# Later modulation pieces in the first bodies of three phases, and an earlier wait for the context latent

## The chip, the cores and the metric

The kernel runs on one core of one Trainium2 chip. The metric is the device time of one execution in microseconds; the comparison is between the medians of several executions of the kernel before and of the changed one.

## What is computed

All arithmetic is float32 on 256 tokens of width 2048. Two blocks follow one another. Cut to what matters here:

```python
# first block
h = x + hybrid_mixer(rms_norm(x), w_in, ...)                  # ends with @ w_out
h = h + memory_cross_attention(rms_norm(h), rms_norm(mem), wq, wk, wv, wo)
h = h + square(relu(rms_norm(h) @ mlp_w1)) @ mlp_w2
x = rms_norm(h)
# second block: its modulation depends on c, c_ctx and w_mod alone, not on x
sh1, sc1, gt1, sh2, sc2, gt2 = split(silu(c) @ w_mod + b_mod, 6)
csh1, csc1 = first two of split(silu(c_ctx) @ w_mod + b_mod, 6)
h  = rmsnorm(x) * (1 + sc1) + sh1
hc = rmsnorm(ctx) * (1 + csc1) + csh1
cq, ckv, kr, qn, kn, vn, f = split_columns(h @ w_in)
ckv_c, kr_c, kn_c, vn_c = those columns of hc @ w_in
kv_c = rmsnorm(ckv_c, g_kv) @ w_ukv                           # "context latent"
...                                                           # attentions, fourier mix, conv_ffn
```

`w_mod` is 2048 x 12288. Because the product with it needs nothing of the first block, it is computed beside the first block's big matrix products.

## The kernel before, in words

All weight matrices lie in one stream of 906 **slots** of 128 x 1024 float32 (512 KB), in the order in which they are used. A **phase** (`Phase`, in the table `PH`) is one matrix product over a run of slots. A **block** of a phase is 256 output columns; for a product over 2048 inputs it has 4 slots. Phases run in **bodies**: memk, memv, wq, wo and all w1 and w2 phases have two bodies of 16 slots each.

Each slot passes through five hands, in this order on each of them:

- SyncE (`load`, L362) brings it from HBM into one of 8 `raw` buffers, once the slot eight earlier has been split.
- ScalarE (`slot`, L1015) rounds it to the upper part `whi`, one of 4 buffers, once TensorE has done the slot four earlier.
- VectorE (`slot`, L1597) subtracts: lower part `wlo` = `raw` - `whi`.
- TensorE (`phase`, L485) does 24 matmuls on a slot: weights upper x input upper, upper x lower, lower x upper.
- ScalarE and VectorE take the finished block out of PSUM (`evac_fn` in `over`), three slots later (`LAG`).

Nothing but the order of the instructions on each engine sets the schedule. `over` writes that order for ScalarE and VectorE. It makes the first three slots (`PRE`) of a phase in the **tail** of the phase before, beside the steps called `tail(j)`. In the tails of wout, memv and wo these steps are the normed input of the next phase: ScalarE makes an upper quarter of `act` (L1106, `upper_after`), VectorE the lower quarter (L1703, `lower_after`), four of them. wout and wo are residual phases: the block taken out is added to `h` (L1654) and squared by ScalarE (L1093); the squares are summed on VectorE (L1642, L1723). The last quarter on ScalarE is queued behind the last square, and the upper parts of slots 3 to 6 of the next phase behind that quarter. TensorE starts slot n of the first block only with quarter n of the input and with its own `wlo`.

**The modulation.** The product with `w_mod` runs over 24 bodies, those of memk to w2_3. In each, VectorE makes 16 **pieces** (`mod_chunk`): a piece multiplies 128 x 512 of `w_mod` by one column of silu(c) and adds it to `modacc`; piece 0 is L1581, the others L1583. In the 8 bodies of memk to wo a piece is done twice, once for c and once for c_ctx; in the w1 and w2 bodies once. The table `MOD_AT` says which pieces stand at which slot of a body; the first piece of an entry stands ahead of that slot's `wlo`, the others behind it. From the second modulated body on, piece 0 comes behind a copy of the last body's result out of PSUM (L1560). TensorE sums `modacc` over the partitions behind slot 12 of the body (L505, `MOD_OUT_AT`), once piece 15 is done.

Two pieces share one load of 512 KB into one of two `modraw` buffers (L368). On SyncE's queue one such load follows every two loads of slots, and it waits until the pair of pieces two earlier is done (`mod_used`). SyncE works in order, so a waiting modulation load holds up the slots behind it.

GpSimd issues a load of 2 MB, the context (L404), when the first block of w1_0 has been taken out.

**The context latent.** In the second block, `ckv_c` normed is the input of phase kn_c, slots 588 to 591. ScalarE makes its upper part (`latent_upper`, L1438) and VectorE its lower part (`latent_lower`, L2219), both in the tail of kr_x behind the third slot made ahead for kn_c (j = 2). They go to chunks 0 to 3 of `act`. kr_x, the phase before, has two slots of 8 chunks each: the first reads chunks 0 to 7 of `act`, the second chunks 8 to 15. In that tail VectorE also has `latent_part(2)` (L2195), the sum of the squares of another latent.

```python
MOD_AT = ((0, 1), (2,), (3,), (4,), (5,), (6,), (7,), (8, 9), (10,), (11,), (12,), (13,), (14,), (15,))
...
for k in ks[:1]:
    mod_chunk(ph, i, k)
ve.wait_ge(hi_done, i * ph.S + (at + 1))
ve.tensor_tensor(wlo[...], raw[...], whi[...], ALU.subtract).then_inc(split_done, 1)
for k in ks[1:]:
    mod_chunk(ph, i, k)
```

Of the kernel before, what the change touches and what calls it, by code (L numbers as in the profile page):

```python
# [37 lines left out]
RAW_N, SPL_N, MOD_N = 8, 4, 2  # L38
# [55 lines left out]
MOD_BODIES = 24  # L94
MOD_CTX = 8
MOD_AT = ((0, 1), (2,), (3,), (4,), (5,), (6,), (7,), (8, 9), (10,), (11,), (12,), (13,), (14,), (15,))

MOD_OUT_AT = 12
PRE = 3
PH, N_SLOTS = phases()  # L100
# [26 lines left out]
def build(nc, x_t, mem_t, ctx_t, stream, mods, pvec, eye, cmix, catt, na_bias, na_mask, out_t):  # L127
    es = ExitStack()
    with es:
# [3 lines left out]
        def sem(name):  # L133
            return es.enter_context(nc.semaphore(name))
# [101 lines left out]
        slot_used = sem("slot_used")  # L236
# [768 lines left out]
        def _(sc):  # L1005
# [429 lines left out]
            def latent_upper(n, c0, src):  # L1435

                sc.wait_ge(lat_normed, n + 1)
                sc.activation(act[:, 0, c0:c0 + LC, :], src, ACT.Copy).then_inc(lat_hi, 1)  # L1438
# [62 lines left out]

            def context_latent_upper(j):
                if j == 2:
                    sc.wait_ge(slot_used, SPL_N + PH["kr_x"].slot0 + PH["kr_x"].slots)
                    latent_upper(0, 0, ckv[:, 1, :, :])
            phase("ckv_c", to(ckv[:, 1, :, :]), both_sqrt)
            phase("kr_c", one(kr[:, 1, :]), second_sqrt)
# [15 lines left out]
            phase("ckv_x", to(ckv[:, 0, :, :]), local("ckv_x"), into("cq"))  # L1523
            phase("cq", to(cq), local("cq"), into("kr_x"))
            phase("kr_x", one(kr[:, 0, :]), local("kr_x"), into("kn_c", context_latent_upper))
            phase("kn_c", to(kN[:, :, 1, :]), local("kn_c"), into("v_c"))
            phase("v_c", to(mlaV[:, 1, :, :], flip=True), local("v_c"), into("kn_x"))
# [18 lines left out]
        def _(ve):  # L1546
# [15 lines left out]
            def mod_chunk(ph, i, k):  # L1562

                mb = i + ph.mod0
                q = k // 2
                if k % 2 == 0:
                    ve.wait_ge(mod_in[q % MOD_N], mb * 64 + 16 * (q // MOD_N + 1))
                if k == 0:
                    if mb:
                        mod_store(mb, 2 if mb <= MOD_CTX else 1)  # L1570
                elif k % 2 == 0:
                    ve.wait_ge(mod_used, mb * 8 + (k // 2 + MOD_N))
                else:
                    ve.wait_ge(dve_step, mod_mark[k - 1])
                for w in range(ph.mod):
                    wt = modraw[:, q % MOD_N, (k % 2) * MOD_COL:(k % 2 + 1) * MOD_COL]
                    at = C_SILU + DC * w + k
                    col = small[:, at:at + 1]
                    acc = modacc[:, w, :]
                    if k == 0:  # L1580
                        ins = ve.tensor_scalar(acc, wt, col, None, ALU.mult)  # L1581
                    else:
                        ins = ve.scalar_tensor_tensor(acc, wt, col, acc, ALU.mult, ALU.add)  # L1583
                if k % 2:
                    ins.then_inc(mod_used, 1)
                else:
                    chain.tick(ins)
                    mod_mark[k] = chain.now()

            def slot(ph):  # L1590
                def f(i, j):
                    at = ph.slot0 + j
                    ks = MOD_AT[j] if ph.mod and j < len(MOD_AT) else ()
                    for k in ks[:1]:
                        mod_chunk(ph, i, k)
                    ve.wait_ge(hi_done, i * ph.S + (at + 1))
                    ve.tensor_tensor(wlo[:, at % SPL_N, :], raw[:, at % RAW_N, :], whi[:, at % SPL_N, :].bitcast(F32),  # L1597
                                     ALU.subtract).then_inc(split_done, 1)
                    for k in ks[1:]:
                        mod_chunk(ph, i, k)  # L1600
                return f
# [879 lines left out]
```

## Time and profile before

| | us |
|---|---|
| median of 3 runs | 2903.57 |
| lowest, highest | 2901.63, 2904.53 |
| the profiled execution, its own time | 2901.38 |
| span of its trace | 2899.6 |
| TensorE busy | 2817.0 |
| VectorE busy | 2066.1 |
| ScalarE busy | 1357.9 |

The profiled execution took 1.8 us more than its span, which lies outside the trace. Times of rows count from the start of the span. In the trace PE is TensorE, DVE VectorE, ACT ScalarE, POOL GpSimd, and SPq the queue of SyncE. In a timeline the columns are start, duration, engine, line, operation, what it writes from what, shape and count, and in brackets the idle time ahead of it and who ended it. Two instructions of an engine overlap a little in the records: a `wlo` lasts 1.22 us, but the next instruction is shown to start 1.13 us after it.

### The profile page before, as it was taken

Reading aid. Unit: us, or ns where it says so; the run is one execution under the profiler, and the core shown is the slowest. Engines: PE = TensorE matmul, PEld = TensorE weight load, DVE = VectorE, ACT = ScalarE, POOL = GpSimd, SP = SyncE. Lnnn points to the kernel's source line nnn. Section 1 sums busy time; section 2 is a strip of 40 time slices with the busy share of each in tenths; the row PEclk is TensorE's granted clock in tenths of the full one; section 3 lists DMA queues with packets and bytes.
Section 4 is the critical chain, followed back from the end, with each engine's and each line's share of the span. In section 5 each row is a group of like instructions: output and inputs, shape, how many; then the busy total and the mean of one; then the engine's idle time right before and its main releaser. Section 6 shows DMA issues by size and latency. Waiting matters only on the chain.

```text
span 2899.6 us, 55174 instructions
## 1 busy us (share of the span) xinstructions
PE 2817.0 (97%) x23814; PEld 2768.6 (95%) x23814; DVE 2066.1 (71%) x2866; ACT 1357.9 (47%) x1723; POOL 4.6 (0%) x12
## 2 busy tenths in 40 slices
PE   7999998999999999999999999999989999999998
PEld 7999998999999999999999999997789999999998
DVE  7988755888869787787777866545566665675675
ACT  4445453444434553544545545455445544553453
POOL 0000000000000000000000000000000000000000
PEclk9999998999999999999999999999999999999999
DMA  6555204678747777777777765433245566556553
GB/s 237 182 175 165 68 8 155 209 275 288 261 152 250 288 279 279 285 282 283 293 275 273 277 219 189 163 122 124 89 149 199 194 198 191 194 188 201 191 188 124
DMA packets 160516, 591.59 MB, mean 204 GB/s; under 512 B 17840, under 2 KB 17840, under 8 KB 159760
## 3 DMA queue, kind: packets, MB, share of 16 engines
q1 hardware_dynamic: 159408, 580.45, 57.9%
q0 software_dynamic: 864, 7.60, 0.7%
q8 instruction: 188, 3.08, 0.4%
q14 instruction: 56, 0.46, 0.1%
HBM read 585.88 MB, written 2.10 MB: 203 GB/s over the span
## 4 chain that ended last, share of the span: by engine, by line
PE 88%; DVE 7%; ACT 2%; issue 1%; DMA 1%; SPq 0%; DVEq 0%; ACTq 0%
PE bank L485 79%; DVE wlo L1597 2%; PE bank L827 1%; DVE modacc L1583 1%; PE bank L690 1%; PE bank L505 1%; ACT whi L1015 1%; PE bank L704 1%; PE bank L522 1%; PE bank L526 1%; PE bank L795 1%; PE bank L805 1%; DVE tmp L1776 0%; PE bank L794 0%; PE bank L514 0%
## 5 line engine op out<-in xcount | busy, mean ns | idle before, releaser
L485 PE MATMUL bank<-act,whi 128*128 128x256 f32 x10144 | 1765.2, 280 | 44.3 <-DVE wlo L1597 28.7
L485 PEld LDWEIGHTS bank<-act,whi 128*128 128x128 f32 x10144 | 1546.3, 190 | 50.2 <-DVE wlo L1597 25.8
L1597 DVE TENSOR_TENSOR wlo<-raw,whi 128x1024 fp32r<-128x1024 f32 x906 | 1096.5, 1222 | 453.0 <-ACT whi L1015 450.9
L485 PE MATMUL bank<-act,wlo 128*128 128x256 f32 x5072 | 1413.9, 279 | 0.0
L1015 ACT ACTIVATE whi<-raw 128x1024 fp32r<-128x1024 f32 x906 | 943.3, 1057 | 779.2 <-PE bank L485 778.5
L485 PEld LDWEIGHTS bank<-act,wlo 128*128 128x128 f32 x5072 | 962.5, 190 | 0.0
L485 PE MATMUL bank<-hid,whi 128*128 128x256 f32 x3456 | 590.2, 277 | 1.5 <-DVE wlo L1597 1.5
L485 PEld LDWEIGHTS bank<-hid,whi 128*128 128x128 f32 x3456 | 520.8, 188 | 1.9 <-DVE wlo L1597 1.3
L485 PE MATMUL bank<-hid,wlo 128*128 128x256 f32 x1728 | 478.2, 277 | 0.0
L1583 DVE SCALAR_TENSOR_TENSOR modacc<-modraw,small,modacc 128x512 f32<-128x512 f32 x480 | 348.3, 746 | 18.9 <-DMA modraw<-mods 13.6
L485 PEld LDWEIGHTS bank<-hid,wlo 128*128 128x128 f32 x1728 | 324.9, 188 | 0.0
L485 PE MATMUL bank<-whi,act 128*128 128x256 f32 x896 | 156.8, 279 | 0.2 <-ACT kN L1027 0.2
L485 PEld LDWEIGHTS bank<-whi,act 128*128 128x128 f32 x896 | 136.3, 188 | 0.5 <-ACT kN L1027 0.4
L485 PE MATMUL bank<-wlo,act 128*128 128x256 f32 x448 | 124.6, 278 | 0.0
L1679 DVE SCALAR_TENSOR_TENSOR ev<-bank,pv,ev 128x255 f32<-128x255 f32 x176 | 76.9, 478 | 63.2 <-ACT ev L1080 61.6
L1832 DVE SCALAR_TENSOR_TENSOR modacc<-cin,pv,modacc 128x256 f32<-128x256 f32 x232 | 98.4, 477 | 0.0
L485 PEld LDWEIGHTS bank<-wlo,act 128*128 128x128 f32 x448 | 84.1, 188 | 0.0
L1093 ACT ACTIVATE ev<-h 128x512 f32<-128x512 f32 x32 | 20.2, 632 | 124.1 <-DVE h L1654 78.8
L1080 ACT ACTIVATE ev<-bank,pv 128x256 f32<-128x256 f32 x88 | 44.9, 560 | 70.6 <-PE bank L485 70.6
L1668 DVE TENSOR_TENSOR hid<-ev,hid 128x512 fp32r<-128x512 f32 x32 | 22.1, 692 | 64.9 <-ACT hid L1069 64.9
L1085 ACT ACTIVATE ev<-ev 128x256 f32<-128x256 f32 x44 | 18.4, 418 | 80.1 <-DVE ev L1679 80.1
L1066 ACT ACTIVATE ev<-bank 128x512 f32<-128x512 f32 x32 | 19.1, 598 | 53.2 <-PE bank L485 53.2
(363 smaller groups left out, 1519.5 us busy)
## 6 DMA issues: line engine op xcount, KB each, us to landing
raw<-stream SPq DMA_DIRECT2D x906, 512.0 KB, 4.6
modraw<-mods SPq DMA_DIRECT2D x192, 512.0 KB, 4.5
h<-x_t SPq DMA_DIRECT2D x4, 512.0 KB, 5.2
memV<-mem_t POOLq DMA_DIRECT2D x1, 2048.0 KB, 8.5
tmp<-ctx_t POOLq DMA_DIRECT2D x1, 2048.0 KB, 9.7
out_t<-tmp SPq DMA_DIRECT2D x4, 512.0 KB, 2.6
cz<-catt POOLq DMA_DIRECT2D x1, 1216.0 KB, 11.6
bias<-na_bias POOLq DMA_DIRECT2D x1, 1024.0 KB, 5.2
```

The source lines that it names most:

```text
L485: mm = pe.matmul(b[:, hf * T:(hf + 1) * T], lhs, rhs, start=(kc == 0 and hf == 0 and n == 0), stop=(kc == ph.chunks - 1 and n == 2), skip_ ...
L505: mm = pe.matmul(bank[2][:, 4 * w + n:4 * w + n + 1], modacc[:, w, n * P:(n + 1) * P], ones[:, 0:1], start=True, stop=True, skip_group_che ...
L522: return pe.matmul(out, src[:, tok], ones[:, 0:1], start=start, stop=stop, skip_group_check=True)
L526: return pe.matmul(out, small[:, col + n:col + n + 1].to_broadcast([P, P]), ident[:, :], start=start, stop=True, skip_group_check=True)
L690: mm = pe.matmul(bk(hg, 0)[:, n, :], MT[hg][:, n, :], X[hg][:, n, :], start=True, stop=True)
L704: mm = pe.matmul(bk(hg, 2)[:, n, :], XT[hg][:, n, :], Y[hg][:, n, :], start=True, stop=True)
L1015: sc.activation(whi[:, at % SPL_N, :], raw[:, at % RAW_N, :], ACT.Copy).then_inc(hi_done, 1)
L1080: ins = sc.activation(ev[:, 0, hf * T:(hf + 1) * T], b2(b)[:, hf, :], ACT.Identity, scale=par("ff_conv", n * 6 + (6 * first + 3 * hf + 1)) ...
L1583: ins = ve.scalar_tensor_tensor(acc, wt, col, acc, ALU.mult, ALU.add)
L1597: ve.tensor_tensor(wlo[:, at % SPL_N, :], raw[:, at % RAW_N, :], whi[:, at % SPL_N, :].bitcast(F32), ALU.subtract).then_inc(split_done, 1)
L1679: ins = ve.scalar_tensor_tensor(o, b2(b)[:, hf, so], par("ff_conv", n * 6 + (6 * first + 3 * hf + j)), o, ALU.mult, ALU.add)
L1832: ins = ve.scalar_tensor_tensor(acc, x_, w, acc, ALU.mult, ALU.add)
```

## The change

`MOD_LATE` names memk, wq and w1_0. In their first body the pieces follow a second table: none stands at slots 0 to 2, and the 16 pieces stand at slots 3 to 13, two at some of them. Their second bodies and all other phases keep `MOD_AT`.

In the tail of kr_x, ScalarE's upper part of the context latent waits for the first slot of kr_x instead of for both.

```diff
 MOD_AT = ((0, 1), (2,), (3,), (4,), (5,), (6,), (7,), (8, 9), (10,), (11,), (12,), (13,), (14,), (15,))
+MOD_LATE = {"memk", "wq", "w1_0"}
+MOD_LATE_AT = ((), (), (), (0, 1), (2, 3), (4,), (5, 6), (7,), (8, 9), (10,), (11, 12), (13,), (14,), (15,))
...
             def context_latent_upper(j):
                 if j == 2:
-                    sc.wait_ge(slot_used, SPL_N + PH["kr_x"].slot0 + PH["kr_x"].slots)
+                    sc.wait_ge(slot_used, SPL_N + PH["kr_x"].slot0 + 1)
                     latent_upper(0, 0, ckv[:, 1, :, :])
...
                     at = ph.slot0 + j
-                    ks = MOD_AT[j] if ph.mod and j < len(MOD_AT) else ()
+                    table = MOD_LATE_AT if ph.name in MOD_LATE and i == 0 else MOD_AT
+                    ks = table[j] if ph.mod and j < len(table) else ()
```

Instructions move on VectorE alone; the order on TensorE, ScalarE, SyncE and GpSimd is the same. In the changed kernel the lines stand two or three further down: the `wlo` line is L1600 there, the piece L1585, the lower quarter L1706, the residual L1657.

VectorE in the tail of wout and the first slots of memk, before: from the `wlo` of slot 0 of memk on.

```order
L1597 TENSOR_TENSOR wlo<-raw,whi 128x1024
L1583 SCALAR_TENSOR_TENSOR modacc<-modraw,small,modacc 128x512 x2
L1703 TENSOR_TENSOR act<-tmp,act 128x1024
L1583 SCALAR_TENSOR_TENSOR modacc<-modraw,small,modacc 128x512 x2
L1597 TENSOR_TENSOR wlo<-raw,whi 128x1024
L1703 TENSOR_TENSOR act<-tmp,act 128x1024
L1583 SCALAR_TENSOR_TENSOR modacc<-modraw,small,modacc 128x512 x2
L1597 TENSOR_TENSOR wlo<-raw,whi 128x1024
L1703 TENSOR_TENSOR act<-tmp,act 128x1024
L1654 TENSOR_TENSOR h<-bank,h 128x512
```

And now, from the lower quarter behind the same `wlo` to the `wlo` of slot 4:

```order
L1706 TENSOR_TENSOR act<-tmp,act 128x1024
L1600 TENSOR_TENSOR wlo<-raw,whi 128x1024
L1706 TENSOR_TENSOR act<-tmp,act 128x1024
L1600 TENSOR_TENSOR wlo<-raw,whi 128x1024
L1706 TENSOR_TENSOR act<-tmp,act 128x1024
L1657 TENSOR_TENSOR h<-bank,h 128x512
L1645 TENSOR_TENSOR stat<-stat,ev 128x512
L1706 TENSOR_TENSOR act<-tmp,act 128x1024
L1726 TENSOR_TENSOR stat<-stat,ev 128x512
L1583 TENSOR_SCALAR modacc<-modraw,small 128x512 x2
L1600 TENSOR_TENSOR wlo<-raw,whi 128x1024
L1585 SCALAR_TENSOR_TENSOR modacc<-modraw,small,modacc 128x512 x4
```

The four pieces that stood ahead of the residual add now stand behind it, and behind them two pieces, not one, lie between some neighbouring `wlo`.

VectorE in the first body of w1_0, before: from the last lower quarter to the `wlo` of slot 5.

```order
L1703 TENSOR_TENSOR act<-tmp,act 128x1024
L1723 TENSOR_TENSOR stat<-stat,ev 128x512
L1583 SCALAR_TENSOR_TENSOR modacc<-modraw,small,modacc 128x512
L1597 TENSOR_TENSOR wlo<-raw,whi 128x1024
L1583 SCALAR_TENSOR_TENSOR modacc<-modraw,small,modacc 128x512
L1597 TENSOR_TENSOR wlo<-raw,whi 128x1024
L1583 SCALAR_TENSOR_TENSOR modacc<-modraw,small,modacc 128x512
L1597 TENSOR_TENSOR wlo<-raw,whi 128x1024
```

And now, the same stretch from the sum behind that quarter on:

```order
L1726 TENSOR_TENSOR stat<-stat,ev 128x512
L1562 COPY msum<-bank 128x2x4
L1583 TENSOR_SCALAR modacc<-modraw,small 128x512
L1600 TENSOR_TENSOR wlo<-raw,whi 128x1024
L1585 SCALAR_TENSOR_TENSOR modacc<-modraw,small,modacc 128x512 x2
L1600 TENSOR_TENSOR wlo<-raw,whi 128x1024
L1585 SCALAR_TENSOR_TENSOR modacc<-modraw,small,modacc 128x512 x2
L1600 TENSOR_TENSOR wlo<-raw,whi 128x1024
```

The copy of the last result and piece 0 moved to slot 3, where piece 4 stood.

## Rows read from the trace of the kernel before

**Rows 1.** The page's busy times; a piece of the chain that ended last

```profile
PE 2817.0 (97%) x23814; PEld 2768.6 (95%) x23814; DVE 2066.1 (71%) x2866; ACT 1357.9 (47%) x1723; POOL 4.6 (0%) x12
...
1049.50 43.54 PE bank L485 x384
```

**Rows 2.** TensorE's waits over the span: total, times, longest

```profile
PE bank L485 <- DVE wlo L1597: 30.2, 16, 7.7
```

**Rows 3.** Timeline of VectorE, first body of memk

```profile
543.28 0.88 DVE L1581 TENSOR_SCALAR modacc<-modraw,small 128x512 f32<-128x512 f32 x2
...
554.86 0.68 DVE L1654 TENSOR_TENSOR h<-bank,h 128x512 f32<-128x512 f32 x1
...
557.26 1.23 DVE L1703 TENSOR_TENSOR act<-tmp,act 128x1024 fp32r<-128x1024 f32 x1 [1.12 <-ACT act L1106]
...
560.33 1.22 DVE L1597 TENSOR_TENSOR wlo<-raw,whi 128x1024 fp32r<-128x1024 f32 x1
...
562.79 1.22 DVE L1597 TENSOR_TENSOR wlo<-raw,whi 128x1024 fp32r<-128x1024 f32 x1
...
585.61 1.41 DVE L1583 SCALAR_TENSOR_TENSOR modacc<-modraw,small,modacc 128x512 f32<-128x512 f32 x2
```

**Rows 4.** Timeline of TensorE, same body; the stretch 561.40 to 564.80 with its clock (0.50)

```profile
561.61 0.80 PE L485 MATMUL bank<-act,whi 128*128 128x256 f32 x2 [3.54 <-DVE wlo L1597]
...
591.71 1.84 PE L505 MATMUL bank<-ones,modacc 128*128 128x1 f32 x16
...
561.40:564.80 3.40, 3.19 (x15) 3.19 (x16) 3.40 (x6) 0.00 (x0) 0.00 (x0) 0.50 0.26 84
```

**Rows 5.** Timeline of ScalarE, same body

```profile
555.57 0.63 ACT L1093 ACTIVATE ev<-h 128x512 f32<-128x512 f32 x1 [6.76 <-DVE h L1654]
...
557.06 3.88 ACT L1015 ACTIVATE whi<-raw 128x1024 fp32r<-128x1024 f32 x4
```

**Rows 6.** Timelines of VectorE and (last row) TensorE, first body of wq

```profile
732.02 0.17 DVE L1560 COPY msum<-bank 128x8 f32<-128x8 f32 x1 [1.77 <-PE bank L505]
...
742.54 2.35 DVE L1703 TENSOR_TENSOR act<-tmp,act 128x1024 fp32r<-128x1024 f32 x2
...
764.54 1.41 DVE L1583 SCALAR_TENSOR_TENSOR modacc<-modraw,small,modacc 128x512 f32<-128x512 f32 x2 [0.90 <-DMA modraw<-mods]
...
768.34 1.22 DVE L1597 TENSOR_TENSOR wlo<-raw,whi 128x1024 fp32r<-128x1024 f32 x1
...
770.51 0.39 PE L485 MATMUL bank<-act,whi 128*128 128x256 f32 x2
```

**Rows 7.** First body of w1_0: VectorE, TensorE, GpSimd, SyncE; 986 to 996 with DMA rate last

```profile
969.00 1.22 DVE L1703 TENSOR_TENSOR act<-tmp,act 128x1024 fp32r<-128x1024 f32 x1 [2.06 <-ACT act L1106]
...
986.71 0.75 DVE L1583 SCALAR_TENSOR_TENSOR modacc<-modraw,small,modacc 128x512 f32<-128x512 f32 x1 [5.17 <-DMA modraw<-mods]
...
972.68 0.50 PE L485 MATMUL bank<-act,whi 128*128 128x256 f32 x2 [2.48 <-DVE wlo L1597]
...
1000.80 0.40 PE L485 MATMUL bank<-act,whi 128*128 128x256 f32 x2
...
976.62 0.53 POOL L404 DMA_DIRECT2D tmp<-ctx_t  x1 [523.25 <-ACT ev L1066]
...
977.36 0.33 SPq L368 DMA_DIRECT2D modraw<-mods  x1
...
986.00:996.00 10.00, 9.39 (x80) 9.21 (x79) 9.21 (x12) 5.40 (x7) 0.00 (x0) 1.00 1.03 392
```

**Rows 8.** Tail of kr_x and start of kn_c: ScalarE, VectorE, TensorE

```profile
1925.91 1.06 ACT L1438 ACTIVATE act<-ckv 128x1024 fp32r<-128x1024 f32 x1 [0.33 <-PE bank L485]
...
1926.75 1.91 DVE L2195 TENSOR_REDUCE tmp<-tmp 128x256 f32<-128x1024 f32 x1
1928.57 1.22 DVE L2219 TENSOR_TENSOR act<-ckv,act 128x1024 fp32r<-128x1024 f32 x1
...
1929.85 0.56 PE L485 MATMUL bank<-act,whi 128*128 128x256 f32 x2 [3.98 <-DVE act L2219]
```

## The prediction, made before the changed kernel ran

> **What bounds the kernel now.** Start with the busy times on the page: TensorE works 2817.0 of 2899.6 us [rows 1], so only its idle time, some 82 us, can be won by reordering. Next, its waits by releaser: 30.2 us of idle are 16 waits of L485 for a lower part on VectorE [rows 2]. Then the timelines show where those waits are and what VectorE did in them. The pace of TensorE is in the chain: 384 matmuls, 16 slots, take 43.54 us, 2.72 per slot [rows 1].
>
> First body of memk: TensorE waits 3.54 us for the lower part of slot 3 [rows 4], and in the 3.4 us after the wait its granted clock is 0.50, 1.2 GHz [rows 4]. The wait comes from VectorE. It reaches the residual add L1654 at 554.86 [rows 3], though the last slot of wout left TensorE near 549.6 (from the wait's start at 558.07 back by three slots of 2.72 and by 0.22, a gap too small for a row). Behind the add hang ScalarE's square at 555.57, its last quarter, and the upper parts from 557.06 [rows 5], then VectorE's last quarter at 557.26 and the lower part of slot 3 at 560.33 [rows 3]. Ahead of the add stand four modulation pieces.
>
> First body of wq: TensorE does not wait. Slot 11 gets its lower part at 768.34 + 1.22 = 769.56 and starts at 770.51 [rows 6], so 0.95 us is left. First body of w1_0: a wait of 2.48 us at slot 3 and a wait of VectorE of 5.17 us for a modulation load [rows 7]. Start of kn_c: 3.98 us for the lower part of the context latent [rows 8].
>
> **Prices of the parts.** A doubled piece with the `wlo` behind it takes 562.79 - 560.33 = 2.46 us [rows 3]. Two quarter subtractions, the same size as a `wlo`, end 2.35 after the start of the first with 1.22 for the last, so one takes 1.13 [rows 6]. A doubled piece is then 1.33, a single one half, 0.67. Piece 0 doubled is 0.79 (shown as 0.88, less the overlap of 0.09) [rows 3].
>
> **memk, first body.** Pieces 0 to 3 leave the tail: 0.79 + 3 x 1.33 = 4.78 us. The add comes at 554.86 - 4.78 = 550.1, behind the end of wout, so the whole shift is usable. The last quarter follows at 557.26 - 4.8 = 552.5, its sum of squares 1.13 later, then piece 0 (0.79, new there in place of a piece of 1.33) and the lower part of slot 3 from 555.0 to 556.2. TensorE is ready for slot 3 at about 557.8, so the 3.54 goes, with 0.22 of an earlier gap of the same sort. The half clock goes too: 3.4 us at half speed lost 1.7. Together 5.5 us.
>
> What is late next is VectorE. Between 543.28 and piece 15 it is idle for only 1.12 us, at the last quarter [rows 3], and that wait for ScalarE stays. The work to the end of piece 15 is the same, so piece 15 still ends at 585.61 + 1.33 = 586.9. The pieces moved behind slot 3 push the lower parts of slots 5, 7, 9 and 11 past TensorE's need. The lower part of slot 12 stands ahead of piece 15 and behind piece 14 in both tables; it ends near 585.7, TensorE does the slot in 2.72 and comes to the modulation sum at about 588.7, where it stood at 591.71 [rows 4]. So 3.0 us remain. I take 0.4 off for loads (below): **-2.6**. Bounds: -5.5, if VectorE were never late, and 0, if loads eat the rest.
>
> **wq, first body.** Here nothing is to be won and VectorE loses head start: while TensorE works through the tail, VectorE now waits for upper parts where it did pieces. Pieces can begin only behind the last quarter, which ends at 742.54 + 2 x 1.13 = 744.8, or 1.33 earlier, 743.5, without the piece ahead of it. From there to the `wlo` of slot 11 stand the copy (0.08), piece 0, pieces 1 to 13 and the `wlo` of slots 3 to 10: 0.08 + 0.79 + 13 x 1.33 + 8 x 1.13 = 27.2, so that `wlo` runs 770.7 to 771.9, against a need at 770.5 [rows 6]. Loss 1.5 us. **Loads** come on top. A pair of pieces has one modulation load, and two loads of slots are queued behind it on SyncE, three of 524 KB. At slots 3 to 8 VectorE wants a pair each 3.8 us (2 pieces and a `wlo`); the old table wanted one each 4.9 (two `wlo`). At the rate of 392 GB/s of 986 to 996 [rows 7] the three take 4.0 us. Four such intervals lose 0.2 each, and before there was already one wait of 0.90 for a load in this body [rows 6], which had slack to hide in and now has none. Loads: +0.8. **wq +2.3**, bounds 0 (slack as before) and +5 (each of four loads 0.9 late).
>
> The Trainium skill, page "DMA: Bandwidth & Descriptors", section "Specifications", puts the HBM limit of a core at about 358 GB/s. By that the three loads would take 4.4 us, 0.6 late at four intervals, and wq and memk would each cost about 1.6 us more: a sum of +4.1 instead of +0.9. The trace's 392 GB/s over ten microseconds is above that figure, so I go by the trace.
>
> **w1_0, first body.** Pieces are single. The copy and pieces 0 to 3 leave the tail: 0.08 + 0.39 + 3 x 0.67 = 2.5 us. The last quarter moves from 969.00 [rows 7] to 966.5, and behind it, with the sum, copy and piece 0, the lower part of slot 3 is ready near 969.9; TensorE is ready at 972.68 - 2.48 = 970.2 [rows 7]. The 2.48 goes, just. Slower here is SyncE: the load for pair 2 can leave only after piece 1, now behind slot 3's `wlo`, near 970.6, that for pair 3 near 973.1, pair 4 near 976.7 and pair 5 near 980; pair 5's left at 977.36 [rows 7]. GpSimd's 2 MB of context is issued at 976.62 [rows 7], and now about 977.0, since the upper part of slot 6, whose load is later, stands ahead of the take-out that releases it. Beside it pair 5's load landed 9.3 us after issue, just ahead of the piece at 986.71 that waited 5.17 us for it [rows 7]. Now pair 4's and its two slots are caught by it as well. I expect piece 8 near 986.5 and slot 8 on TensorE at 988 to 989, due at 984.7; then pair 5, three transfers of 1.3 us behind, makes slot 9 wait another microsecond. Slot 12 starts at 1001 to 1005, where it stood at 1000.80 [rows 7]. **+1.2**, bounds -3.1 (2.48 and the 0.6 us by which slot 8 was late go, nothing comes) and +4.2.
>
> **kr_x.** ScalarE's order is unchanged; L1438 stands behind the upper part of the third slot and was idle for just 0.33 us ahead of it [rows 8]. That much earlier it starts. But the lower part L2219 begins at 1928.57 because VectorE is in L2195 until then (1926.75 and 1.91 long); L1438 had ended at 1926.97 [rows 8]. The queue ahead of L2219 ends the wait, not L1438. **0.0**; bounds 0 and -0.33.
>
> **Sum.** -2.6 + 2.3 + 1.2 + 0 = +0.9 us. On the profiled execution (2901.38, that is the span and 1.8) this gives 2902.3; that execution was 2.2 below the median of the three runs, so the median goes to 2903.57 + 0.9 = **2904.5**.
>
> **Rivals.**
> - *Nothing is given back.* memk -5.5, wq 0, w1_0 -3.1: -8.6, 2895. It needs VectorE to have room in memk and wq; 1.12 us idle in 43 us [rows 3] and 0.95 us of lead [rows 6] speak against. 0.04.
> - *The latent was held by ScalarE.* If the order on VectorE were not what holds L2219, the 3.98 and about 1.7 of half clock behind it would go: 0.9 - 5.7 = -4.8, 2899. Against it stand L2195's own two rows. The change then also does what its words say, which I hold it does not in effect. 0.04.
> - *Slower: loads set the pace of the pieces.* Place: SyncE's queue in the three first bodies. If three transfers take 5.0 us at the tight intervals instead of 4.0, each of four intervals costs 1.2 instead of 0.2: memk and wq 4 more each, w1_0 at its bound 4.2: 0.9 + 8 + 3 = +12, 2915. It decides from about 4.5 us per three loads (+5.8 in all). For: a load landed 9.3 us after its issue with the context beside it, and one wait of 0.90 stood in wq at the slow pace. Against: 392 GB/s. 0.12.
> - The forecast: 0.80, from 2898.5 to 2909.5 by the bounds taken together.
>
> **How the numbers follow.** About 0.2%, 5.8 us, is what a measurement of this kernel can tell from no change. The forecast and the latent rival lie within it, but for 0.01 at either edge of the forecast; the first rival is faster, the last slower. Faster 0.05, same 0.82, slower 0.13. The range for 8 in 10 leaves out the far rivals: 2899 to 2910.
>
> **What would show it.** In the changed profile: no wait of TensorE at slot 3 of memk and no half clock there, but small waits of 0.2 to 1.1 us at slots 5 to 11, and the modulation sum near 588.7; waits at slots 9 and 11 of wq, sum 2 us later against slot 0; in w1_0 no wait at slot 3, one of 3 to 4 us at slot 8; at kn_c the same 4 us. The prediction is wrong if VectorE shows idle time between the pieces of memk other than for loads, or if the modulation waits for loads exceed about 4 us in memk and wq together.

## The result

| | us |
|---|---|
| kernel before, median of 17 runs | 2904.97 (2900.83 to 2907.60) |
| changed kernel, median of 17 runs | 2909.81 (2905.97 to 2913.78) |
| ratio of the two, 95% interval | 1.0018 (1.0012 to 1.0025) |
| profiled execution of the changed kernel, its own time | 2907.19 |
| span of its trace | 2905.4 |

The ratio is +5.2 us, and its interval excludes no change. The forecast was a loss of 0.9 us, one that a measurement would not tell from no change. The sign is right, the loss is nearly six times as large, and it is clear of the scatter. The median lies 0.2 us inside the range of 2899 to 2910.

Two rows of the changed kernel's page and of its waits over the span, TensorE's busy time and its waits for lower parts (total, times, longest), against [rows 1, 2]:

```profile
PE 2818.1 (97%) x23814; PEld 2768.2 (95%) x23814; DVE 2067.7 (71%) x2866; ACT 1357.9 (47%) x1723; POOL 4.6 (0%) x12
```

```profile
PE bank L487 <- DVE wlo L1600: 34.7, 21, 8.3
```

The busy times agree with those before to within 2 us; the waits for a `wlo` grew from 30.2 us in 16 to 34.7 in 21. The loss is best read stage by stage. The table has the time from the start of slot 0 to the start of slot 12 on TensorE, each from the first matmul of the slot in the trace:

| first body of | before | after | difference | predicted |
|---|---|---|---|---|
| memk | 39.72 | 38.41 | -1.31 | -2.6 |
| wq | 32.65 | 35.80 | +3.15 | +2.3 |
| w1_0 | 38.92 | 41.99 | +3.07 | +1.2 |

At kn_c nothing changed. The sum is +4.9; the rest of the 5.8 us between the two profiled executions is small differences ahead of memk (0.5 by slot 0) and between the stages. Times of rows of the changed kernel are read against those of before after subtracting what it is ahead or behind at the start of the stage: +0.50 in memk, -0.71 in wq, +2.73 in w1_0, +5.87 at kn_c.

**memk.** Timeline of VectorE in the changed kernel, from the residual add to the first pieces; its order is that of the prediction, its times within 0.1 us of it:

```profile
550.58 0.68 DVE L1657 TENSOR_TENSOR h<-bank,h 128x512 f32<-128x512 f32 x1
...
552.98 1.23 DVE L1706 TENSOR_TENSOR act<-tmp,act 128x1024 fp32r<-128x1024 f32 x1 [1.12 <-ACT act L1108]
...
555.52 1.22 DVE L1600 TENSOR_TENSOR wlo<-raw,whi 128x1024 fp32r<-128x1024 f32 x1
556.65 2.92 DVE L1585 SCALAR_TENSOR_TENSOR modacc<-modraw,small,modacc 128x512 f32<-128x512 f32 x4
559.49 1.22 DVE L1600 TENSOR_TENSOR wlo<-raw,whi 128x1024 fp32r<-128x1024 f32 x1
```

The add, 554.86 before [rows 3], stands at 550.58 - 0.50 = 550.1, the `wlo` of slot 3 begins at 555.0 where it began at 560.33. The wait of 3.54 and the half clock behind it [rows 4] are gone. Then the stretch of slot 3 (its columns: busy time of PE, PEld, DVE, ACT, POOL, then granted clock, DMA share, GB/s), and the modulation sum on TensorE:

```profile
558.20:561.90 3.70, 3.70 (x35) 3.70 (x34) 3.70 (x5) 0.00 (x0) 0.00 (x0) 1.00 0.76 279
```

```profile
591.00 1.84 PE L507 MATMUL bank<-ones,modacc 128*128 128x1 f32 x16
```

The sum is at 591.00 - 0.50 = 590.5, not at 588.7: of the 3.0 us that VectorE's work was to leave, 1.8 are gone. One row shows where a part of them went: four instructions, two doubled pieces, take 559.49 - 556.65 = 2.84, not 2 x 1.33 = 2.66. The waits of the body:

```profile
PE bank L487 <- DVE wlo L1600: 2.5, 3, 1.1
...
DVE modacc L1585 <- DMA modraw<-mods: 1.0, 2, 0.6
```

**wq.** VectorE from piece 0 on, against [rows 6], and TensorE at slots 9 and 11:

```profile
742.87 0.88 DVE L1583 TENSOR_SCALAR modacc<-modraw,small 128x512 f32<-128x512 f32 x2
743.65 1.22 DVE L1600 TENSOR_TENSOR wlo<-raw,whi 128x1024 fp32r<-128x1024 f32 x1
744.79 2.93 DVE L1585 SCALAR_TENSOR_TENSOR modacc<-modraw,small,modacc 128x512 f32<-128x512 f32 x4
747.64 1.22 DVE L1600 TENSOR_TENSOR wlo<-raw,whi 128x1024 fp32r<-128x1024 f32 x1
...
759.60 1.42 DVE L1585 SCALAR_TENSOR_TENSOR modacc<-modraw,small,modacc 128x512 f32<-128x512 f32 x2 [0.39 <-DMA modraw<-mods]
...
771.36 1.22 DVE L1600 TENSOR_TENSOR wlo<-raw,whi 128x1024 fp32r<-128x1024 f32 x1
...
772.98 1.41 DVE L1585 SCALAR_TENSOR_TENSOR modacc<-modraw,small,modacc 128x512 f32<-128x512 f32 x2 [0.40 <-DMA modraw<-mods]
```

```profile
766.18 0.50 PE L487 MATMUL bank<-act,whi 128*128 128x256 f32 x2 [0.82 <-DVE wlo L1600]
772.63 0.50 PE L487 MATMUL bank<-act,whi 128*128 128x256 f32 x2 [0.74 <-DVE wlo L1600]
```

From piece 0 to the `wlo` of slot 11 VectorE takes 771.36 - 742.87 = 28.5, where the prediction counted 27.1 without loads. Slot 11 starts at 772.63 + 0.71 = 773.3 instead of 770.51: 2.8 late.

**w1_0.** VectorE, TensorE, SyncE and GpSimd, against [rows 7]:

```profile
969.07 1.23 DVE L1706 TENSOR_TENSOR act<-tmp,act 128x1024 fp32r<-128x1024 f32 x1 [2.07 <-ACT act L1108]
...
971.28 1.22 DVE L1600 TENSOR_TENSOR wlo<-raw,whi 128x1024 fp32r<-128x1024 f32 x1
...
990.67 0.75 DVE L1585 SCALAR_TENSOR_TENSOR modacc<-modraw,small,modacc 128x512 f32<-128x512 f32 x1 [5.58 <-DMA modraw<-mods]
...
995.18 1.22 DVE L1600 TENSOR_TENSOR wlo<-raw,whi 128x1024 fp32r<-128x1024 f32 x1
```

```profile
979.04 0.33 SPq L370 DMA_DIRECT2D modraw<-mods  x1
979.50 0.53 POOL L406 DMA_DIRECT2D tmp<-ctx_t  x1 [527.25 <-ACT ev L1068]
992.70 0.76 PE L487 MATMUL bank<-act,whi 128*128 128x256 f32 x2 [4.54 <-DVE wlo L1600]
```

The wait at slot 3 is gone. The load for pair 4, issued at 979.04, 0.46 us ahead of the 2 MB of context, lets piece 8 begin only at 990.67, 11.6 us later, and slot 8 waits 4.54 us. Behind that wait the clock falls (stretch of slot 8, columns as above):

```profile
992.60:997.60 5.00, 4.90 (x24) 4.93 (x25) 3.78 (x6) 3.10 (x5) 0.00 (x0) 0.53 1.00 394
```

Slot 8 takes 4.95 us. The `wlo` of slot 9 had ended at 995.18 + 1.22 = 996.4; slot 9 starts at 997.65, so here the half clock itself cost 1.25.

**kn_c.** Upper part, sum of squares, lower part, TensorE, against [rows 8]:

```profile
1931.35 1.05 ACT L1440 ACTIVATE act<-ckv 128x1024 fp32r<-128x1024 f32 x1
```

```profile
1932.62 1.90 DVE L2198 TENSOR_REDUCE tmp<-tmp 128x256 f32<-128x1024 f32 x1
1934.44 1.21 DVE L2222 TENSOR_TENSOR act<-ckv,act 128x1024 fp32r<-128x1024 f32 x1
```

```profile
1935.71 0.62 PE L487 MATMUL bank<-act,whi 128*128 128x256 f32 x2 [3.97 <-DVE act L2222]
```

ScalarE's upper part starts 0.4 us earlier (1925.48 against 1925.91), the lower part where it did (1928.57), and the wait is 3.97.

### The profile page after: what moved, and what is told of

It is laid out like the page before. It is cut to its first block, busy times and chain, and to the rows that moved or that the text cites. A ratio compares the mean times of both kernels' runs of the same rounds, so it can differ in the third digit from the quotient of the medians.

```text
span 2905.4 us, 55175 instructions
## 1 busy us (share of the span) xinstructions
PE 2818.1 (97%) x23814; PEld 2768.2 (95%) x23814; DVE 2067.7 (71%) x2866; ACT 1357.9 (47%) x1723; POOL 4.6 (0%) x12
## 4 chain that ended last, share of the span: by engine, by line
PE 86%; DVE 9%; ACT 2%; DMA 2%; issue 1%; SPq 0%; DVEq 0%; ACTq 0%
PE bank L487 76%; DVE wlo L1600 3%; DVE modacc L1585 2%; PE bank L829 1%; DMA modraw<-mods 1%; PE bank L692 1%; PE bank L507 1%; ACT whi L1017 1%; DVE ev L1619 1%; PE bank L706 1%; PE bank L524 1%; PE bank L528 1%; PE bank L797 1%; DVE modacc L1835 1%; PE bank L807 1%
## 5 line engine op out<-in xcount | busy, mean ns | idle before, releaser
L1600 DVE TENSOR_TENSOR wlo<-raw,whi 128x1024 fp32r<-128x1024 f32 x906 | 1096.1, 1221 | 458.2 <-ACT whi L1017 456.1
L1585 DVE SCALAR_TENSOR_TENSOR modacc<-modraw,small,modacc 128x512 f32<-128x512 f32 x480 | 348.1, 746 | 19.8 <-DMA modraw<-mods 14.2
```

## The experiments

All kernels keep the line numbers of the kernel before. Each gives one execution's trace beside the times. "Late" is the second table of the change. Stage times are again from slot 0 to slot 12.

### One part of the change at a time

Late pieces in memk alone, in wq alone, in w1_0 alone, each with the old wait for the latent; then the new wait alone, with an empty set. The first of the four against the changed kernel:

```diff
-MOD_LATE = {"memk", "wq", "w1_0"}
+MOD_LATE = {"memk"}
...
-                    sc.wait_ge(slot_used, SPL_N + PH["kr_x"].slot0 + 1)
+                    sc.wait_ge(slot_used, SPL_N + PH["kr_x"].slot0 + PH["kr_x"].slots)
```

> Late pieces in memk's first body alone; wq, w1_0 and the latent's wait as before. Theory A (each body pays its own sum, and what it costs is loads: memk -1.3, wq +3.2, w1_0 +3.3 in the changed kernel's trace, added up to its +5.2): memk reaches the modulation sum behind slot 12 at 590.4 to 591, 1 to 1.5 us sooner than before counted from memk's slot 0, nothing else moves, the time is 1.3 us below the kernel before. Rival B (what is won in memk is lost later whatever the other bodies do, since VectorE falls behind): the gain at the modulation sum is gone by the end of wo, and the time is the same or above.

> Late pieces in wq's first body alone. Theory A: TensorE reaches slot 12 of wq 3.0 to 3.3 us later against slot 0 than before, with waits at slots 7 to 12, and keeps that to the end: +3.2 us. Rival B (wq loses only because memk's late body left it in another state of loads): less than 1.5 us is lost.

> Late pieces in w1_0's first body alone. Theory A: no wait at slot 3 (-2.6 us), a wait of 4 to 5 us at slot 8 for a modulation load issued just ahead of the 2 MB of context, then half clock; in all +3.0 to +3.6 us. Rival B (the wait at slot 8 comes from the shift of wq and memk, the 2 MB falling on another load): -3 to +1 us.

> The context latent's earlier wait alone, no late pieces. Theory A (VectorE's sum L2195 holds the lower part): ScalarE's upper part starts 0.1 to 0.4 us earlier, L2219 at the same distance from kn_c, TensorE waits 4.0 us as before, time within 0.3 us of before. Rival B (ScalarE's wait held it): TensorE's wait of 4.0 us shrinks by 1 us or more and the time falls by 1 to 5.6 us.

| | median | ratio to before, 95% | own stage |
|---|---|---|---|
| memk alone | 2902.28 | 0.9993 (0.9983 to 1.0002) | 39.08, before 39.72 |
| wq alone | 2908.29 | 1.0011 (1.0002 to 1.0020) | 36.52, before 32.65 |
| w1_0 alone | 2907.93 | 1.0009 (1.0000 to 1.0018) | 43.28, before 38.92 |
| latent alone | 2903.68 | 1.0000 (0.9991 to 1.0009) | wait 3.97, before 3.98 |

Each ratio here and below is against the kernel before as measured beside it on the same chip. The four ratios add up to +0.13%, the whole change has 0.18%. With 0.09% of uncertainty on each of the four this says little by itself. The stages say more: a first body with the old table in wq takes 32.65 us whatever memk and w1_0 do, and each body with the late table moves the way that it moves in the changed kernel. The parts do not draw on each other. By the ratios wq and w1_0 each lose some 3 us, and memk wins 2, with an interval that still holds no change.

The sizes did not come as expected. wq alone loses 3.9 us in its stage, not 3.0 to 3.3, with 1.5 us of waits for loads where the changed kernel has 0.8. w1_0 alone loses 4.4, not 3.0 to 3.6: the wait at slot 8 is the same, 4.55, but slot 7 waits 0.5 as well, and slot 8 takes 5.26 us instead of 4.95. memk alone reaches the modulation sum only 0.45 us sooner than the kernel before, not 1 to 1.5.

In the trace of the new wait alone (VectorE and TensorE):

```profile
1926.28 1.90 DVE L2195 TENSOR_REDUCE tmp<-tmp 128x256 f32<-128x1024 f32 x1
1928.10 1.21 DVE L2219 TENSOR_TENSOR act<-ckv,act 128x1024 fp32r<-128x1024 f32 x1
...
1929.37 0.80 PE L485 MATMUL bank<-act,whi 128*128 128x256 f32 x2 [3.97 <-DVE act L2219]
```

This execution is 0.47 us ahead at kr_x, so all three stand where they did. L2219 starts when L2195, ahead of it on VectorE, is done, as before: that L2195 holds it is shown.

The kernels with the old table in memk give its scatter. From slot 0 to slot 12 they take 39.72 (before), 40.98 (wq alone), 40.38 (w1_0 alone), 39.65 (latent alone), and 40.84 and 40.36 in two kernels below: mean 40.3. The cause is the wait at slot 3 and the half clock behind it: without that wait and that slot, the rest of the stage takes 30.8 to 31.1 us in all six. Slot 3 lasts 5.18 us in the kernel before and 6.52 with late pieces in wq alone, behind the same wait (stretch of that slot there, then its first matmul):

```profile
560.95:567.47 6.52, 6.51 (x32) 6.51 (x33) 6.52 (x9) 0.98 (x2) 0.00 (x0) 0.53 0.60 219
```

```profile
560.96 0.80 PE L485 MATMUL bank<-act,whi 128*128 128x256 f32 x2 [3.53 <-DVE wlo L1597]
```

The late table in memk takes 38.41 (the changed kernel), 39.08, and 39.79 and 38.91 below: mean 39.0. So by the means late pieces win 1.3 us in memk, not 2.6.

### The context load out of the way

GpSimd waits for four more blocks before it issues the 2 MB of context; once in the changed kernel, once in the kernel before:

```diff
-            pool.wait_ge(block_free, FREE + PH["w1_0"].block0 + 1)
+            pool.wait_ge(block_free, FREE + PH["w1_0"].block0 + 5)
```

> The changed kernel, with GpSimd's 2 MB of context issued four blocks of w1_0 later (behind block 4 instead of block 0). Theory A (the context beside the late modulation loads makes the wait at slot 8): from slot 1 to slot 13 of w1_0 the cost of +3.2 to +4.4 us over before is gone and turns into a gain of 0 to 3 us, loads for pairs 4 and 5 land within 6 us of issue instead of 10.5 to 11.6; the whole kernel 3 to 6 us below the changed one. Rival B (three loads per pair of pieces are too much at this pace in any case): the wait at slot 8 shrinks by less than half.

> The kernel before, with the context issued four blocks later. Theory A: VectorE's wait of 5.17 us for a modulation load goes, TensorE's wait of 0.61 us at slot 8 of w1_0 goes, and with it 0.5 to 1.5 us from slot 1 to slot 13; the wait of 2.5 us at slot 3 stays. Rival B (that load was late for other reasons): it still lands 7 us or more after its issue.

Changed kernel with the later load: 2904.10, 0.9996 (0.9986 to 1.0005). Kernel before with it: 2903.92, 0.9992 (0.9982 to 1.0002). First body of w1_0: 36.40 us against 41.99 in the changed kernel; in the kernel before 39.51 against 38.92. The waits in that body of the changed kernel, from 965 to 1010, first as it is, then with the later load:

```profile
DVE modacc L1585 <- DMA modraw<-mods: 9.9, 5, 5.6
...
PE bank L487 <- DVE wlo L1600: 4.5, 1, 4.5
```

```profile
DVE modacc L1583 <- DMA modraw<-mods: 5.9, 5, 2.1
...
PE bank L485 <- DVE wlo L1597: 0.9, 2, 0.7
```

So it is the context load that turns the late table's gain in w1_0 into a loss. With the context early the late table is worth +3.1 us (41.99 against 38.92). With the context late it is worth -3.1 (36.40 against 39.51), or -2.5 if it is read against the kernel before itself. With the old table the later load brings nothing, where a gain was expected. VectorE's wait for pair 5 does shrink from 5.17 [rows 7] to 1.3, but it had cost TensorE only 0.6 us at slot 8; and slot 3, behind the same wait as before, took 5.2 us in this execution instead of 3.66. These 1.5 us of lower clock hide what the later load may bring to the old table, and they are part of the -3.1; no run here separates them. memk (39.79) and wq (36.02) of the changed kernel stay as they were.

### Small modulation loads

Both kernels with modulation loads of 128 columns instead of 1024. The pieces still run over the whole buffer, so VectorE's work is the same, but they read old data and the modulation is not computed:

```diff
-                sp.dma_start(modraw[:, q % MOD_N, :], mods[ds(body * 4 + q, 1), :, :]...
+                sp.dma_start(modraw[:, q % MOD_N, 0:128], mods[ds(body * 4 + q, 1), :, 0:128]...
```

> The changed kernel, each modulation load cut to an eighth (the first 128 of 1024 columns); the pieces work on what lies in the buffer otherwise, so the modulation is not computed. Orders and waits are the same. Theory A (my sum was right but for the loads): slot 1 to slot 13 of memk -3.0 us against before, of wq +1.2 to +1.8 us (VectorE's lost head start alone), of w1_0 -2 to 0 us. Rival B (VectorE's order alone makes the whole loss): wq stays at +3 us, memk at -1.3.

> The kernel before with the same cut loads, the modulation is not computed: the pair to the run with late pieces and cut loads. Theory A: memk and wq from slot 1 to slot 13 within 0.5 us of the kernel before, since there no wait of TensorE hung on a load; w1_0 0.5 to 1 us less. Rival B: memk or wq changes by more than 1 us, then loads also set the old table's pace.

Changed kernel with small loads: 2900.86, 0.9988 (0.9978 to 0.9998). Kernel before with them: 2904.66, 0.9999 (0.9989 to 1.0010).

| slot 0 to 12 | memk | wq | w1_0 |
|---|---|---|---|
| old table, small loads | 40.14 | 32.65 | 39.37 |
| late table, small loads | 37.64 | 35.03 | 37.01 |
| late less old | -2.5 | +2.4 | -2.4 |

The loads cost the old table nothing and the late one 1.2 us in memk (-1.3 instead of -2.5), 1.1 in wq (+3.5, the mean of 35.80, 36.52 and 36.02 less 32.65, instead of +2.4) and over 5 in w1_0. With no wait of a piece for its load in the traces of memk and wq the late table still loses 2.4 us in wq. VectorE's order alone does that, and it does more than the 1.2 to 1.8 expected from the lost head start. In w1_0 the old table's slot 3 ran at the lower clock in this execution (5.1 us), which is in its 39.37 and so in the -2.4.

### Two phases only, and a softer table

These kernels keep the parts that pay. First, late pieces in memk and w1_0, the old wait, and the later context load:

```diff
-MOD_LATE = {"memk", "wq", "w1_0"}
+MOD_LATE = {"memk", "w1_0"}
...
-            pool.wait_ge(block_free, FREE + PH["w1_0"].block0 + 1)
+            pool.wait_ge(block_free, FREE + PH["w1_0"].block0 + 5)
```

> The late table in memk and w1_0 alone, the old wait for the latent, and the 2 MB context load released four blocks later. Theory A (what the late table costs is wq's lost head start and, in w1_0, the context load in the way; without both, the two phases keep what they win): memk about -1.1 us from its slot 1 to its slot 13, the mean of the runs so far, wq 0, w1_0 -2.4 as in the changed kernel with the later context load; together -3.5 us, a ratio near 0.9988. Rival B (the phases draw on each other: a later residual and a later end of the modulation in memk and w1_0 is given back behind them, or the later context load costs elsewhere): the stages show their gains but slot 0 of w2_0 and up_0 stand less than 2 us ahead of the kernel before, a ratio of 0.9995 or more.

Then a softer table, which leaves pieces 0 and 1 in the tail and has three pairs of pieces without a `wlo` between, not five; in memk alone:

```diff
-MOD_LATE = {"memk", "wq", "w1_0"}
-MOD_LATE_AT = ((), (), (), (0, 1), (2, 3), (4,), (5, 6), (7,), (8, 9), (10,), (11, 12), (13,), (14,), (15,))
+MOD_LATE = {"memk"}
+MOD_LATE_AT = ((0, 1), (), (), (2, 3), (4,), (5,), (6, 7), (8,), (9, 10), (11,), (12,), (13,), (14,), (15,))
```

> A softer table for the first body of memk alone: pieces 0 and 1 stay at slot 0, ahead of the residual add, pieces 2 to 15 stand at slots 3 to 13, with three adjacent pairs of pieces instead of five. wq, w1_0 and the latent as before. The residual add comes 2 x 1.33 = 2.66 us earlier than before, so a wait of 3.54 - 2.66 = 0.9 us is left at slot 3. Theory A (what memk can win is set by VectorE's total work up to the lower part of slot 12, and each adjacent pair adds 0.19): slot 12 is late by the same VectorE work as in the late table but for two pairs, so memk gives -2.5 to -3.0 from slot 1 to slot 13, or -0.5 us more than the late table. Rival B (VectorE's total doesn't set the end; the waits for the loads that the dense pieces ask for do): with pair 2's load asked for some 5 us earlier there is no wait for a load, and memk gives -3.5 or more. Rival C: the half clock stays in spite of the short wait, and memk gives -1 or less.

Then the softer table in memk, the late one in w1_0 and the later context load. `MOD_LATE_AT` holds a table for each of the two phases here:

```diff
-                    table = MOD_LATE_AT if ph.name in MOD_LATE and i == 0 else MOD_AT
+                    table = MOD_LATE_AT[ph.name] if ph.name in MOD_LATE and i == 0 else MOD_AT
...
-            pool.wait_ge(block_free, FREE + PH["w1_0"].block0 + 1)
+            pool.wait_ge(block_free, FREE + PH["w1_0"].block0 + 5)
```

> The softer table in memk, the late table in w1_0, the context load released four blocks later, wq and the latent as before. Theory A: the gains add up, memk -2.5 to -3 and w1_0 -2.4: -5 us, a ratio near 0.9982. Rival B: the sum is the same as with the late table in memk, -3.5, since both end at VectorE's work.

And the softer table in wq alone (the table of the second kernel, with `{"wq"}`):

> The softer table in the first body of wq alone: pieces 0 and 1 stay in the tail of memv, pieces 2 to 15 at slots 3 to 13, with three adjacent pairs instead of five. memk, w1_0 and the latent as before. Theory A (the late table costs wq the VectorE work moved behind the last quarter and 0.19 us for each further adjacent pair): against the late table 0.79 + 1.33 = 2.1 us of pieces and two pairs, 0.4, less lie behind the last quarter, so of the 3.2 to 3.9 us that the late table cost here, 0.7 to 1.4 are left from slot 1 to slot 13, and no more. Rival B (the waits for the loads of dense pieces carry most of the cost in wq, whatever the head start): the pieces from slot 3 on are as dense as in the late table, so 2 to 3 us are lost. The whole against before: A within 1.5 us of it, B +2 to +3.

| | median | ratio to before, 95% | memk | wq | w1_0 |
|---|---|---|---|---|---|
| late memk and w1_0, context later | 2900.06 | 0.9983 (0.9974 to 0.9992) | 38.91 | 32.65 | 37.25 |
| softer memk | 2903.34 | 0.9993 (0.9984 to 1.0002) | 37.52 | | |
| softer memk, late w1_0, context later | 2898.04 | 0.9982 (0.9973 to 0.9991) | 38.00 | 32.65 | 36.00 |
| softer wq | 2905.42 | 1.0002 (0.9993 to 1.0011) | | 34.07 | |

The softer table takes 37.8 us in memk, 1.2 less than the late one and 2.5 less than the old one; more than the 0.5 expected from two pairs. The waits for loads shrink with it, from 1.0 us in the changed kernel to 0.6 and 0.2. A wait at slot 3 is left, 0.51 us in one trace and 1.36 in the other, and slot 3 takes 4.07 us behind either, not the 5.1 to 6.5 of the old table; its granted clock is 1.00 in both. VectorE and TensorE of softer memk at slot 3, then VectorE's wait for loads from 543 to 600:

```profile
558.56 1.22 DVE L1597 TENSOR_TENSOR wlo<-raw,whi 128x1024 fp32r<-128x1024 f32 x1
559.69 2.93 DVE L1583 SCALAR_TENSOR_TENSOR modacc<-modraw,small,modacc 128x512 f32<-128x512 f32 x4
```

```profile
559.83 0.51 PE L485 MATMUL bank<-act,whi 128*128 128x256 f32 x2 [0.51 <-DVE wlo L1597]
```

```profile
DVE modacc L1583 <- DMA modraw<-mods: 0.6, 2, 0.3
```

Against the mean of the old table, 40.3, the two kernels win 2.8 and 2.3. That is at and just under the 2.5 to 3.0 expected if VectorE's work up to slot 12 sets the end, and not the 3.5 or more if the loads did. For the whole run the interval of the softer memk alone still holds no change.

In wq the softer table loses 34.07 - 32.65 = 1.4 us, the upper end of the 0.7 to 1.4 expected if the pieces behind the last quarter set the cost, and outside the 2 to 3 expected if the loads did. Over the whole run it shows no difference, 1.0002. Two waits for a load stand in it as with the late table (1.1 us here, 0.8 in the changed kernel), so loads explain little of the difference between the two tables, 2.0.

The kernel with the softer table in memk, the late one in w1_0 and the later context load is faster than the kernel before: 2898.04 against 2904.64, 0.18% less by the ratio. So is the first of this group, by 0.17%. Their intervals all but coincide, so which of these two is better stays open.

## Why the prediction was right or wrong

The direction of each stage was right, and TensorE waited where it was to wait. The steps that failed are three prices, each set too low: the doubled piece at 1.33 us wherever it stands, 0.4 us for the loads in memk, and the +1.2 of w1_0, which left out the half clock behind the new wait at slot 8 and put the load that it waits for too early.

**What bounds the kernel, and the edits' own times: right.** In memk the residual add, the last quarter and the `wlo` of slot 3 came within 0.1 us of the times worked out (550.1, 552.5 and 555.0). In w1_0 the last quarter was put at 966.5 and stood at 969.07 - 2.73 = 966.3; the `wlo` of slot 3 was to be ready near 969.9 and was at 969.8. The order on VectorE and durations of rows give such times well.

**kr_x: right.** 0.0, by the queue ahead of L2219. The rival in which ScalarE held the latent is refuted by the new wait alone.

**The pieces' price: wrong.** The step "a doubled piece is then 1.33" was taken from a piece with a `wlo` behind it, and multiplied by 13. Where two pieces follow each other directly, they take 2.77 to 2.85 instead of 2.66. The kernel before has such a row, in its timeline of VectorE in wq, that the prediction did not use:

```profile
757.12 2.93 DVE L1583 SCALAR_TENSOR_TENSOR modacc<-modraw,small,modacc 128x512 f32<-128x512 f32 x4
759.96 1.22 DVE L1597 TENSOR_TENSOR wlo<-raw,whi 128x1024 fp32r<-128x1024 f32 x1
```

Each piece waits for its forerunner by a semaphore; with a `wlo` between, that wait is over in time. That this wait is the cause is read from the code, not tried. It is also the sign that the prediction named against itself, idle time of VectorE between pieces other than for loads, though each gap is too small for a row. The late table makes five such pairs ahead of slot 11. The old one has one in wq and none in memk, where short instructions stand in between. In wq the five rows of the changed kernel sum to 14.1 where 5 x 2.66 = 13.3 was counted: +0.8. With the 1.5 of lost head start this is 2.3, and the small loads measured 2.4. The sum of memk lacks the same 0.8.

**The loads: right in wq, too small in memk.** wq was given 0.8; its trace has waits of 0.39 (ahead of the `wlo` of slot 8) and 0.40 (ahead of that of slot 12) and a gap of 0.1 beside each, 1.0 in all. So wq is 1.5 + 0.8 + 1.0 = 3.3, measured 3.15, with the waits at slots 9 and 11 that were to show it. memk was given 0.4 and waited 1.0 in the changed kernel, 1.7 in memk alone, 1.4 with late pieces in memk and w1_0, and 2.2 in the changed kernel with the later context load. So memk is -3.0 + 0.8 + 1.0 = -1.2, measured -1.31. Waits for loads in the two first bodies sum to 1.8 us in the changed kernel, under the 4 us at which the prediction was to be wrong by this term; the rival with +12 did not happen. The transfers were not slow: while three of them were wanted at once with the context, the trace shows 423 GB/s (changed kernel; the last three columns are the clock, the DMA share and GB/s):

```profile
979.00:985.00 6.00, 6.00 (x54) 6.00 (x52) 4.22 (x6) 4.97 (x7) 0.53 (x1) 1.00 1.06 423
```

The Trainium skill, page "Perfetto Trace Analysis", section "Roofline", says that one core alone may draw up to about 120% of the 358 GB/s that the prediction weighed; 423 is 118%, and the trace agrees. By 358 the prediction's sum would have been +4.1, closer to the +5.2 measured. But it needs 2.4 us of waits for loads in each of memk and wq, and the changed kernel has 1.0 and 0.8.

**w1_0: the place right, the size wrong.** The prediction had pair 4's load leave at 976.7 (it left at 979.04 - 2.73 = 976.3) and be caught by the context, and a wait of 3 to 4 us at slot 8, which was 4.54. Its steps, in times of the kernel before: slot 8 at 988 to 989, slot 9 3.7 later (2.72 and another microsecond). With another 9.2 to slot 12, as before, this is 1000.9 to 1001.9. The prediction gave 1001 to 1005, and its term took 1002.0, the low end. Measured: slot 8 at 992.70 - 2.73 = 990.0, slot 9 4.95 later, slot 12 another 8.95 later, 1003.9. So the load landed 1.4 us later than put: piece 8 began at 990.67 - 2.73 = 987.9, not 986.5. Slot 8 was due at 992.70 - 4.54 - 2.73 = 985.4, not at 984.7, so the reading of that due time was off as well, though only the size of the wait hangs on it. And the step left out the half clock behind the new wait, though the prediction had counted one behind 3.54 us in memk. By its `wlo` slot 9 could have started 996.4 - 992.7 = 3.7 after slot 8, just as said; the half clock made it 4.95. Why the load took 11.6 us is seen in the DMA queues from 978 to 992 of the changed kernel (packets, MB, share of the 16 engines; q1 is SyncE's, q0 GpSimd's; then KB and median us to landing):

```profile
q1 hardware_dynamic: 1004, 3.66, 66.0%
q0 software_dynamic: 144, 2.10, 35.2%
...
raw<-stream SPq DMA_DIRECT2D x4, 512.0 KB, 12.4
tmp<-ctx_t POOLq DMA_DIRECT2D x1, 2048.0 KB, 10.5
modraw<-mods SPq DMA_DIRECT2D x2, 512.0 KB, 11.1
```

The same stretch with the context elsewhere (softer memk, late w1_0, context later; 975 to 989):

```profile
raw<-stream SPq DMA_DIRECT2D x6, 512.0 KB, 7.1
modraw<-mods SPq DMA_DIRECT2D x3, 512.0 KB, 5.6
```

The sixteen DMA engines are busy throughout in both (66.0% and 35.2% above, 100% of SyncE's queue in the second). The load had been issued, and with the 2.1 MB elsewhere such a load landed in 5.6 us: it is late because the engines carry the context beside it. The Trainium skill, page "DMA: Bandwidth & Descriptors", section "Queues, rings and completion order", says that a DMA engine takes turns between the queues that have work; the trace agrees, in that both moved data side by side, some 0.7 MB each from 982 to 985.

**The chances.** The range held narrowly, and not by its argument: 2909.81 is 0.2 us inside it, and 0.3 above the 2909.5 to which the forecast's own bounds ran. A part of that is the base, whose median of 17 runs is 1.4 us above the 2903.57 used. The 0.82 for "within 0.2%" leaned on terms of opposite sign, -2.6, +2.3 and +1.2, that cancel in the sum. The three errors, 1.3 in memk, 0.9 in wq and 1.9 in w1_0, all went the same way: in all three stages the pieces stand more densely behind slot 3, and what that costs was set too low, in memk by their price and their loads, in wq mostly by their price, in w1_0 by the load and the clock. The 0.2% put as what a measurement can tell from no change was too coarse as well: 17 runs of each kernel gave an interval of 0.13% in all.

## What to carry to other kernels

Price an instruction in the neighbourhood in which it will stand: a row of the same operation next to its own kind, if the trace has one, not a difference taken beside another operation. If every stage of the sum uses that price, its error adds up where the terms seem to cancel. Before work is moved out of a stretch in which its engine would otherwise wait, count that head start as a cost, and before loads are moved in time, look for the large transfer that they will meet; in the changed kernel, moving that transfer took 5.6 us off the first body of w1_0, more than the table won anywhere. A new wait of the bound engine must be priced with the clock behind it.

## What the runs showed of the hardware

The clock behind a like wait is not the same from run to run. In memk a wait of 3.5 us was followed by a slot of 5.18 us in one execution and of 6.52 in another (mean granted clock 0.53, close to 0.50, its lower level of 1.2 GHz). In w1_0 the kernel before waited 2.48 [rows 7] and kept the full clock in the slot behind it; with late pieces in memk alone it waited 2.27 there and the clock fell. In all, behind a wait of 2.3 to 2.5 us at slot 3 of w1_0, the slot took 3.65 or 3.66 us in five executions and 5.1 to 5.3 in three. The stretch of slot 3 of w1_0, first in the kernel before, then in that one:

```profile
972.68:976.34 3.66, 3.66 (x33) 3.66 (x33) 3.54 (x4) 0.60 (x2) 0.00 (x0) 1.00 0.51 182
```

```profile
973.73:978.99 5.26, 5.26 (x33) 5.26 (x33) 3.54 (x4) 0.79 (x3) 0.00 (x0) 0.68 0.68 246
```

Behind the longest of the short waits, 1.43 us at slot 9 of w1_0 in the changed kernel with small loads, the clock stayed at 1.00 (the stretch of that slot):

```profile
992.61:995.55 2.94, 2.94 (x24) 2.94 (x25) 2.94 (x5) 1.50 (x2) 0.00 (x0) 1.00 0.89 298
```

So one profiled execution of the kernel before (39.72 us in memk) is not its typical one (mean 40.3 of six with the same table), and a gain read against it is uncertain by about a microsecond per such wait.
